# A two-block transformer kernel on one core: sublayer boundaries reordered and the prologue rebuilt

## The reference, cut to what matters

```python
mod = (silu(c) @ ada_w[layer] + ada_b[layer])            # vectors of 1024: shift, scale, gate
h = rms_norm(x, g_pre) * (1 + scale) + shift
y = sublayer(h)                                          # e.g. (silu(h @ Wg) * (h @ Wu)) @ W_out
x = x + weight * gate * rms_norm(y, g_post)              # first block
x = x + gate * y                                         # second block: y is not normalised
```

## Time and profile before

| what | value |
|---|---|
| median of 3 runs (lowest, highest) | 2464.57 us (2463.33, 2464.88) |
| the profiled execution's own time | 2460.7 us |
| its span, first to last instruction | 2459.0 us |
| TensorE busy (matmul) | 2231.2 us, 91% |
| VectorE, ScalarE, GpSimd busy | 48%, 39%, 4% |
| mean granted TensorE clock | 0.944 |
| HBM read | 408.47 MB, 167 GB/s over the span |

### The profile page before, as it was taken

How to read it: one execution, slowest core, us unless ns; L and a number is a source line. 1 busy time by engine, 2 the same in 40 slices (tenths; PEclk the granted TensorE clock), 3 DMA queues, 4 the chain that set the end, 5 groups by cost and what they waited for, 6 DMA issues and landing times. The chain is left out here.

```text
span 2459.0 us, 35227 instructions
## 1 busy us (share of the span) xinstructions
PE 2231.2 (91%) x14142; PEld 1870.5 (76%) x14142; DVE 1190.4 (48%) x1891; ACT 960.5 (39%) x1522; POOL 98.2 (4%) x209
## 2 busy tenths in 40 slices
PE   4899898999889998767999799878999999798999
PEld 1798786898788987534898699656777768686997
DVE  0444555444643445554544565685322233665444
ACT  0433523433533335444433543464222123455343
POOL 1100100000100001000000100001000000101000
PEclk7899999999979999778999899999999999999999
DMA  7786586676448774102676332102444343122553
GB/s 280 258 291 255 171 308 240 239 274 244 150 149 281 256 261 136 52 1 86 242 272 247 121 104 86 35 1 86 171 154 154 112 162 98 66 86 74 188 184 120
DMA packets 246604, 411.40 MB, mean 167 GB/s; under 512 B 10221, under 2 KB 191942, under 8 KB 246470
## 3 DMA queue, kind: packets, MB, share of 16 engines
q1 hardware_dynamic: 246470, 409.54, 48.0%
HBM read 408.47 MB, written 1.05 MB: 167 GB/s over the span
## 5 line engine op out<-in xcount | busy, mean ns | idle before, releaser
L991 DVE TENSOR_TENSOR w_lo<-stage,w_hi 128x2048 fp32r<-128x2048 f32 x255 | 585.8, 2298 | 726.0 <-ACT w_hi L616 725.8
L1522 PE MATMUL bank<-h_hi,w_hi 128*128 128x256 f32 (+1 forms) x2432 | 742.6, 305 | 9.1 <-POOL h_lo L589 6.7
L616 ACT CAST w_hi<-stage 128x2048 fp32r<-128x2048 f32 x255 | 484.7, 1902 | 672.9 <-PE bank L1524 258.9
L1523 PE MATMUL bank<-h_lo,w_hi 128*128 128x256 f32 (+1 forms) x2432 | 733.9, 302 | 0.0
L1524 PE MATMUL bank<-h_hi,w_lo 128*128 128x256 f32 (+1 forms) x2432 | 733.2, 301 | 0.0
L1522 PEld LDWEIGHTS bank<-h_hi,w_hi 128*128 128x128 f32 x2432 | 473.6, 195 | 68.4 <-issue 53.4
L1523 PEld LDWEIGHTS bank<-h_lo,w_hi 128*128 128x128 f32 x2432 | 473.6, 195 | 14.8 <-issue 1.2
L1524 PEld LDWEIGHTS bank<-h_hi,w_lo 128*128 128x128 f32 x2432 | 473.2, 195 | 14.1
L1574 PE MATMUL bank<-w_hi,h_hi 128*128 128x512 f32 x776 | 245.9, 394 | 11.4 <-DVE h_lo L1000 8.0
L1574 PE MATMUL bank<-w_hi,h_lo 128*128 128x512 f32 x776 | 243.1, 391 | 0.0
L1574 PE MATMUL bank<-w_lo,h_hi 128*128 128x512 f32 x776 | 243.0, 390 | 0.0
(11 more groups left out here) (187 smaller groups left out, 1933.1 us busy)
## 6 DMA issues: line engine op xcount, KB each, us to landing
ada<-in_ada_w SPq DMA_DIRECT2D x120, 1024.0 KB, 7.0
stage<-in_ffn_w_in SPq DMA_DIRECT2D x88, 1024.0 KB, 6.0
stage<-in_ffn_w_out SPq DMA_DIRECT2D x44, 1024.0 KB, 5.1
stage<-in_ffn_w_gu SPq DMA_DIRECT2D x44, 1024.0 KB, 5.1
stage<-in_ffn_w_down SPq DMA_DIRECT2D x22, 1024.0 KB, 5.1
stage<-in_a_w_in SPq DMA_DIRECT2D x12, 1024.0 KB, 7.7
stage<-in_diff_w_in SPq DMA_DIRECT2D x12, 1024.0 KB, 5.1
ada<-in_kv_ada_w SPq DMA_DIRECT2D x8, 1024.0 KB, 8.4
```

Of the source, the lines that this page charges most:

```text
L616: a.copy(w_hi[:, s, :], stage[:, s, :]).then_inc(hi_done, 1)
L991: v.tensor_tensor(w_lo[:, s, :], stage[:, s, :], w_hi[:, s, :].bitcast(F32), ALU.subtract).then_inc(lo_done, 1)
L1522: m.matmul(dst[:, 0:T], wh, h_hi[:, h0:h0 + T], start=(k == ks[0]), stop=False)
L1523: m.matmul(dst[:, 0:T], wh, h_lo[:, h0:h0 + T], start=False, stop=False)
```

## The change

Prologue: x is the first large transfer, then half of vector 0, then the first three weight units, then the rest of vector 0 and vector 1. x is normalised and transposed before the vectors, weight units 0 and 1 are split before them, and only two vectors stand ahead of the first product. All later vectors move one place on, and the last FFN makes one (`nvec` 1 instead of 0). The context and `w2` are loaded in front of the convolution.

Boundaries: `affine` of tile 0 has its own buffer and moves behind tile 1's residual addition (four blocks of it stand inside tile 1's `x_norm`); `hi` and `lo` work on groups of blocks, (4, 4) for tile 0 and (1, 1, 2, 2, 2) for tile 1, all after tile 1's `x_norm`. `turn(0)` moves behind the last product; with four tiles, `turn(tt - 2)` stands in tile `tt`, and twelve of the sixteen `affine_pair` come after tile 3's `x_norm`. The context's normalisation, `turn` and first `affine_pair` (`first_half`) move to the start of the down products of the FFN before; `turn(1)` for differential attention moves behind the products of tile 2. The ScalarE table for the root is loaded ahead of the down products.

The vectors, the buffer of `affine`'s result and the groups:

```diff
-        N = dict(unit=0, vec=3, chunk=0, bstep=0, silu=0, step=[0, 0, 0])
+        N = dict(unit=0, vec=2, chunk=0, bstep=0, silu=0, step=[0, 0, 0])
...
-        add("ffn", io["ffn_w_gu_2"][1], io["ffn_w_down_2"][1], 256, 0, 29, col_at["norm2_g_2"] + KC, None, one, 11, 2, 11)
+        add("ffn", io["ffn_w_gu_2"][1], io["ffn_w_down_2"][1], 256, 1, 29, col_at["norm2_g_2"] + KC, None, one, 11, 2, 11)
...
-        def h32(k):
-            return mid[:, 4 * D + k * P:4 * D + (k + 1) * P]
+        def h32(s, k, tt):
+            o = D if tt and not s["A"] else 4 * D
+            return mid[:, o + k * P:o + (k + 1) * P]
+
+        def groups(s, tt):
+            return ((0, 4), (4, 4)) if tt == 0 and not s["A"] else ((0, 1), (1, 1), (2, 2), (4, 2), (6, 2))
...
+        def early_half(s):
+            return s is not None and s["kind"] == "diff"
```

SyncE, prologue:

```diff
-            sp.dma_start(w2[:, :, :], io["cmp_w2"].rearrange("k (h p) d -> p (k h) d", p=P)).then_inc(x_landed, 16)
             sp.dma_start(xs[:, 0:2, :], io["x"][0].rearrange("(t p) d -> p t d", p=P)).then_inc(x_landed, 16)
-            sp.dma_start(xs[:, 2:4, :], io["ctx_2"][0].rearrange("(t p) d -> p t d", p=P)).then_inc(x_landed, 16)
-            for v in range(3):
-                load_vec(v, *ada_src(v), 0)
-                load_vec(v, *ada_src(v), 1)
+            load_vec(0, *ada_src(0), 0)
+            for k in range(RING):
+                load_unit(k, subs[0]["w_in"][:, k % 2 * FF + k // 2 * WCOL:k % 2 * FF + (k // 2 + 1) * WCOL].rearrange("(k p) n -> p k n", p=P), KC)
+            load_vec(0, *ada_src(0), 1)
+            load_vec(1, *ada_src(1), 0)
+            load_vec(1, *ada_src(1), 1)
```

GpSimd, `lo` of a group:

```diff
+                pool.wait_ge(act_s, t.at((tag, "hi", k0, tt)))
+                t.done(g.tensor_tensor(h_group(h_lo, s, k0, n, tt), h32_group(s, k0, n, tt),
+                                       h_group(h_hi, s, k0, n, tt).bitcast(F32), ALU.subtract), pool_s, (tag, "lo", k0, tt))
```

ScalarE, the context's half and the boundary (new lines and the context they stand in):

```diff
+            def first_half(prev, s):
+
+                for tt in (2, 3):
+                    x_norm(prev, s, tt)
+                for k in s["ks"][0:5]:
+                    hi_pair(s, k, 1)
...
                 for tt in range(n_prev):
                     y_stats(prev, tt)
+                    if tt == n_prev - 1 and s["T"] == 512:
                         act.wait_ge(w_used, nu)
+                        for k in s["ks"][5:] if early_half(s) else s["ks"][0:2]:
                             hi_pair(s, k, s["cs"][0])
+                    x_norm(prev, s, tt)
+                if n_prev and s["T"] == 256:
+                    for tt in range(2):
+                        for k0, n in groups(s, tt):
+                            hi(s, k0, n, tt)
```

VectorE, `x_norm`, the boundary and the prologue:

```diff
+            def x_norm(s, tt, meanwhile=()):
 
                 tag = f"s{s['n']}"
+                for f in meanwhile[0:1]:
+                    f()
                 mean(1, tt, (tag, "xss", tt, 0), (tag, "xmean0", tt))
+                for f in meanwhile[1:]:
+                    f()
                 inverse(1, tt, (tag, "xroot", tt), (tag, "rstd", tt))
...
                 for tt in range(n_prev):
                     y_update(prev, tt)
+                    if s["T"] == 256:
+                        x_norm(s, tt, one[0:4] if tt == 1 else ())
+                    elif n_prev == 2:
                         x_norm(s, tt)
+                    else:
+                        x_norm(s, tt, pair[0:2] if tt == 2 else pair[2:4] if tt == 3 else ())
+                if n_prev:
+                    for f in one[4:] if s["T"] == 256 else pair if n_prev == 2 else pair[4:]:
+                        f()
                     split(nu + 1)
...
-            for vi in range(3):
+            for tt in range(2):
+                x_norm(subs[0], tt)
+            split(0)
+            split(1)
+            for vi in range(2):
                 vec_row(vi)
                 vec_col(vi)
-            split(0)
-            split(1)
```

TensorE, prologue, down products and what follows them (in differential attention the tiles come in the order 2, 3, 0, 1):

```diff
-            for vi in range(3):
+            for tt in range(2):
+                turn(subs[0], tt)
+            for vi in range(2):
                 vec_acc(vi, 0)
                 vec_acc(vi, 1)
                 vec_sum(vi)
...
                 step(1, None)
                 if s["kind"] in ("nsa", "gqa"):
                     gate(s, tag, 0)
+                if early_half(after_s):
+                    for tt in (2, 3):
+                        turn(after_s, tt)
...
                 def after(tt):
-                    if nxt is None:
-                        return
-                    if tt:
-                        turn(nxt, tt - 1)
-                    elif nxt["T"] // P > n_tiles:
-                        for k in range(n_tiles, nxt["T"] // P):
-                            turn(nxt, k)
-
+                    if nxt and n_tiles == 4 and tt >= 2:
+                        turn(nxt, tt - 2)
...
-                if fills(nxt):
-                    vec_acc(nxt["v"], 0)
                 if nxt:
-                    turn(nxt, n_tiles - 1)
+                    turn(nxt, n_tiles - 2)
+                    if fills(nxt):
+                        vec_acc(nxt["v"], 0)
+                    if not early_half(nxt):
+                        turn(nxt, n_tiles - 1)
...
+                            if w.diff and n == 0 and tt == 2:
+                                turn(s, 1)
```

More of the change, by code:

```diff
@@ L715, in boundary @@
-                    if s and s["T"] == 256 and tt in tiles:
-                        for k in s["ks"]:
-                            hi(s, k, tt)
-                    if s and s["T"] == 512 and n_prev == 2 and tt == 0:
-                        for k in s["ks"][0:5]:
+                    x_norm(prev, s, tt)
+                if n_prev and s["T"] == 256:
+                    for tt in range(2):
+                        for k0, n in groups(s, tt):
+                            hi(s, k0, n, tt)
+                if n_prev and s["T"] == 512:
+                    if not early_half(s):
+                        for k in s["ks"][2:]:
@@ L749, in kv_act @@
                     if n < 2 and s["n"] + 1 < len(subs):
-                        for k in range(KC):
-                            hi(subs[s["n"] + 1], k, n)
+                        for k0, m_ in groups(subs[s["n"] + 1], n):
+                            hi(subs[s["n"] + 1], k0, m_, n)
                     if n in (2, 4):
@@ L976, in turn_over @@
                         gate(s, tag, 0)
+                    if j == 1 and i is None and early_half(nxt):
+                        first_half(s, nxt)
+                nxt = subs[si + 1] if si + 1 < len(subs) else None
+                table(ACT.Sqrt)
                 for_b(act, s, turn_over)
@@ L1091, in affine_pair, with first_half @@
                                        modv[:, s["v0"], 8 * c + k:8 * c + k + 1], ALU.mult, ALU.add), dve_s, (tag, "h32", k, c))
+            def first_half(s):
+                mod_in(s, f"s{s['n']}")
+                for tt in (2, 3):
+                    x_norm(s, tt)
+                for k in s["ks"]:
+                    affine_pair(s, k, 1)
             def boundary(prev, s):
                 n_prev = prev["Td"] // P if prev and prev["bsteps"] else 0
-                tiles = range(s["T"] // P) if s else range(n_prev)
@@ L1097, in boundary @@
-                nu = s["u"] if s else None
-                if s and n_prev:
-                    split(nu)
-                for tt in tiles:
-                    if tt >= n_prev:
-                        x_norm(s, tt)
-                if s and not n_prev and s["T"] == 256:
-                    for tt in tiles:
-                        for k in s["ks"]:
-                            affine(s, k, tt, f"s{s['n']}")
-                if s and not n_prev and s["T"] == 512:
-                    for k in s["ks"]:
-                        affine_pair(s, k, s["cs"][0])
+                if s is None:
+                    for tt in range(n_prev):
+                        y_update(prev, tt)
+                    return
@@ new lines, in boundary @@
+                tag = f"s{s['n']}"
+                nu = s["u"]
+                one = [lambda k=k, tt=tt: affine(s, k, tt, tag) for tt in range(2) for k in range(KC)]
+                pair = [lambda k=k, c=c: affine_pair(s, k, c) for c in (s["cs"][1:] if early_half(s) else s["cs"]) for k in s["ks"]]
+                if n_prev:
+                    split(nu)
+                else:
+                    dve.wait_ge(dve_s, t.at((tag, "A", 0)))
+                    for f in one:
+                        f()
@@ L1382, in _ @@
                 if s["A"] == 0:
-                    mod_in(s, tag)
+                    if not early_half(s):
+                        mod_in(s, tag)
                     if s["kind"] == "kv" and si + 1 < len(subs):
@@ L1847, in _ @@
                 tag = f"s{si}"
-                if si == 0:
-                    pe.wait_ge(dve_s, t.at("cols"))
-                    pe.wait_ge(ada_col, 3)
-                    for tt in range(2):
-                        turn(s, tt)
```

(4 more changed lines are left out.)

184 lines of the change are left out of this document (90 added, 94 removed).

## The result

The changed kernel takes 2424.07 us (median of four runs, 2422.69 to 2426.63); the kernel before, run beside it, takes 2463.95 (2458.58 to 2464.88). The ratio is 0.9844, with a 95% interval from 0.9827 to 0.9861: 39.9 us less. The forecast was 2429.7 us, 34.9 us less by the profile. The profiled execution took 2424.26 us, its span is 2422.3 (before 2459.0), so 36.7 of the gain stands in the two traces. Of the 5.6 us between the forecast and the median, 1.8 are the sum's (span 2424.1 forecast), and the rest is the step from a profile to a median: 3.9 were added, as in the kernel before, but the changed kernel's profiled execution lies at its median.

A forecast was written before the change was run, and what follows sets the result against it. TensorE's matmuls fill 91% of the span, so only its idle time could shrink, chiefly waits on the normalised x. 18.3 - 2.7 + 7.0 + 0.3 + 7.5 + 4.5 = 34.9 us gave 2429.7 us, range 2410 to 2447.

The forecast's parts named there:

- Prologue: Before the first product: transposes earlier, two vectors instead of three; first product at 57.3 instead of 75.60, gain 18.3 us.
- The vector in the last FFN: Vector moved to the last FFN: costs 4.6 us, half falling into idle time at the last boundary; loss 2.7.
- GpSimd's group: A GpSimd subtraction of 512 elements, not in the trace: taken as 1.5 us, bounds 0.80 and 1.69.
- The boundaries with 256 tokens: Five boundaries behind a normalised y: second turn earlier, then GpSimd is late; gain 1.4 us each, 7.0 in all.
- Differential attention: Waits before it fall from 14.2 to 7.9 us, context turns run at full clock; gain 7.5, between 4.5 and 9.6.
- The 2 us of tiles 0 and 1: Before differential attention: these tiles wait some 2 us on eight GpSimd subtractions of 0.80.
- "for a colder first tile": In the differential attention term: half a microsecond deducted from the gain for a first tile at a colder clock.
- Four tiles handed over: Two four-tile boundaries: first turns stop waiting, GpSimd's subtractions come late; gains 2.5 and 2.0, together 4.5, between 0 and 8.
- this collision: VectorE's two residual additions take 2.35 us instead of 1.28 beside GpSimd subtractions; said to leave the sum as it is.
- the rival: At the boundaries the clock stays up: a third of 3.9 us at nine boundaries returns, 12 us more, 2418; chance 0.18.
- the last boundary: The 256-token boundary whose y is not normalised: the same sum as at the other five leaves a gain of 0.3 us.

The follow-up runs named there:

- the run that keeps TensorE busy: Changed kernel plus unused products, 11 (4 in the last FFN) and 11, in the two waits of four 256-token boundaries: 2418.84 us, ratio 0.9806.
- the combined version with GpSimd's order changed: Changed kernel with third weight unit last, unused products at six boundaries and in the prologue, and GpSimd subtracting first-needed blocks first: 2415.11 us, ratio 0.9798.

## Why the prediction was right

**Prologue.** The transposes were predicted at 14.8 and 17.3 and stand at 14.22 and 16.69, the last column at 51.5 (49.65), the first product at 57.3 (55.35). The gain in the trace is 20.25 for 18.3. The tail from the column to the product was right, 5.70 for 5.8. What was mis-sized is the price of the three weight units: the fourth vector unit was put 4.3 us later than before and came 3.2 later (30.89, 27.71), because two of the three transfers lie where the queue waited for a vector buffer; and the eighth came 14.0 us behind it for 14.4. The run with the third unit last shows this: with two units ahead the fourth is used at 27.91. The splits lay beside the transfers, as predicted (ScalarE at 19.78 and 22.78).

**The vector in the last FFN.** A loss of 2.7 was taken. The trace shows 2.1 from the last boundary on, and undoing the move gave 2.8 there. Prologue and vector together: 15.6 predicted, 15.1 and 15.5 measured from the two sides. That this agrees so well is luck: at the first product the lead is 20.6 in both of those comparisons, not 18.3, and 4 to 5 us of it are lost again in stages that the prediction left alone.

**GpSimd's group.** 1.5 us predicted, 1.27 measured, inside the bounds. GpSimd is what is late next, as predicted: its order alone moved the first product by 1.07 us.

**The boundaries with 256 tokens.** The path was right: the second turn comes 3.4 us earlier (3.1 predicted), and then GpSimd is late. The gain was mis-sized: the first product gained 2.2 to 2.3 us at each of the five places for the predicted 1.4. On the scale of the earlier trace rows, which is 20.28 us later (the lead ahead of this boundary), ScalarE's first group is ready at 297.7 (298.1 predicted), and two groups and a block later the product starts at 300.8 (301.6). So 0.46 of the missing 0.85 is the group's price, 1.27 for 1.5, and 0.4 the earlier start. TensorE's idle time fell by 1.3 (6.8 to 5.5), which looks like the predicted 1.4 but isn't that term. The second turn, 1.97 us at half clock before, takes 1.09 in four of the six places and 1.52 in one, but it is not on this path: at 932.02 it still takes 1.97, and the first product comes 9.47 us after the last down product, as at the first boundary.

**Differential attention.** 7.5 predicted; undoing it cost 8.5 against before on its own chip, 6.9 by the two medians. The waits sum to 7.1 us for the predicted 7.9: the context's two turns wait 0.21 and 1.47 (taken as 2.1), the end 4.3 (3.8), since two of the three subtractions ran beside residual additions and took 1.18 and 1.17 and not 0.80; a turn waits 1.1. The 2 us of tiles 0 and 1 came as about 1.1, in waits too short for the list: from 1382.5 to 1384.6 TensorE's steps are 0.69 us apart instead of 0.36. In the traces the stage gained 6.5: 10.5 at its first product, of which 4.0 went within the first 25 steps, to these waits, to tile 1's turn, which now stands among them, and to steps at half clock. The half microsecond "for a colder first tile" was too little.

**Four tiles handed over.** 2.5 and 2.0 predicted. At the first such boundary the product starts 10.4 us after the last down product (10.5 predicted). What the sum left out is behind that start: two late subtractions meet VectorE's splits of weights and take 2.8 us instead of 0.73, and TensorE waits for the last of them inside the product, 1.66 us. The prediction read this collision in the earlier trace rows, asked only whether it meets the 256-token additions, and left the sum as it was; it is the step that failed here. So the waits fell from 10.0 to 9.2, and the traces show a gain of 1.3. At the second such boundary they fell from 10.3 to 7.9, a gain of 3.0. That the two sum to 4.3, for 4.5, is luck.

**The clock.** Over the whole span the records show 273 us at half clock before and 253 after. The prologue's stretches shrank from 51.2 to 30.7, and those of the six 256-token boundaries from 54.4 to 40.8; in sparse attention, behind its boundary, they grew from 75.1 to 88.7. Even so the first product of a boundary still ran at 0.51, as it had at 0.50. So the rival was right in part, that some of the clock comes back by itself; of its price of 3.9 us a boundary, the run that keeps TensorE busy won 1.8 per place. The section of the Trainium skill cited in the prediction (TensorE: Matmul & The Clock Gate, "HAM oscillation — how this bites in real kernels") agrees with this: idle gaps send TensorE back to the low rate.

**The sum.** It was 34.9 by the trace, and the trace gave 36.7. The terms, in us (in the traces: the change of the lead across each place):

| term | predicted | in the traces |
|---|---|---|
| prologue | 18.3 | 20.3 |
| vector in the last FFN | -2.7 | -2.1 |
| five boundaries, 256 tokens | 7.0 | 11.2 |
| the last boundary | 0.3 | 1.5 |
| differential attention | 7.5 | 6.5 |
| four tiles, twice | 4.5 | 4.3 |
| all other stages | 0 | -5.0 |

That the total came so close is thus partly luck: the prologue and the 256-token boundaries gave 7.4 more than predicted, and stages that the sum put at nothing took 5.0. Two of these make up nearly all of it. In sparse attention the lead falls from 29.9 to 26.6. From its first product to its first down product that stage takes 170.9 us in the trace of the kernel before, and 173.8 in the changed kernel's; but it takes 173.4 with the new prologue alone and 173.6 with the boundaries alone, so the loss doesn't hang on either half of the change. Its time doesn't follow the half clock either (80.9 us in the kernel before, 93.6, 83.3 and 94.2 in the others). This stays open. In the FFN behind differential attention 1.6 us go at 1954 us, where a stretch of 3.4 at half clock lies that the kernel before doesn't have; what sends the clock down there was not tried.

## What to carry to other kernels

Price a moved wait by what is late next on every engine behind it; here that named GpSimd and gave the first product's start at a boundary to 0.8 us. Follow that engine past the first product too, and ask which of the other engines' work it will now run beside: the second wait of 1.66 us stood inside a product, behind a subtraction that had met a split of weights. Then price the clock of the work behind the wait: 5.5 us of idle time cost another 1.8 at half clock, and filling them with products that nobody reads saved 7.5 us, where starting 1.07 us earlier saved nothing. A transfer put ahead of a paced queue costs little as long as it fits the queue's own gap (two units, 0.2 us at the fourth vector unit; the third, 3.0), so count gaps before counting bytes. And add up a sum's terms from the trace one by one before trusting its total.

## What was not expected of the hardware

A subtraction of 256 elements on GpSimd takes 0.73 us, and 2.77 to 2.79 beside a VectorE split of weights with two operands of 2048 elements; the split takes 2.65 to 2.83 instead of 2.29. Behind the two waits of 2.75 and 2.72 us the granted clock was 0.51 (1.2 GHz); with unused products in them it was 1.00 (2.4 GHz) throughout, with the first product at the same 9.5 us after the last down product. A product of two 32-bit operands of 128 columns was two instructions in the trace, 44 for 22, where the transposes of the same shape were one each. Stretches at half clock come and go in stages far from an edit: the combined version with GpSimd's order changed has two, at 1307 and 1686 us, that its neighbour lacks.
